# Moving the sliding-window attention out of the delta rule's recurrence and between the levels of its inverses, in a one-core Trainium2 transformer layer

## What is computed

```python
# attention: 8 heads of 64, 2 key/value heads, blocks of 128 queries over 256 keys
s = einsum('bnqhgd,bnkhd->bnhgqk', qb, kb) * HEAD_DIM ** -0.5        # masked to a window of 128
m = maximum(max(s, -1), sink);  p = exp(s - m)
o = einsum('bnhgqk,bnkhd->bnqhgd', p / (sum(p) + exp(sink - m)), vb) # then rms_norm * gain

# delta rule: 4 heads of 128, chunks of 64 tokens
a_mat = strict_lower((k*beta) @ k.T * decay) + I
u, w  = solve(a_mat, [v*beta, k*beta*exp(gc)])        # unit lower triangular, 64 x 64
for each chunk c:                                     # the recurrence, 8 chunks
    v_new = u[c] - w[c] @ state
    o[c]  = q_dec[c] @ state + qk[c] @ v_new
    state = state * decay[c] + k_dec[c].T @ v_new
```

## Time and profile before

| | |
|---|---|
| runs | 1737.12, 1762.24, 1736.94 us; median 1737.12 |
| the profiled execution | 1731.93 us; its span, first to last instruction, 1730.0 us |
| input projection, 0 to 163.0 | TensorE busy 144.1 us |
| `delta_prepare`, 163.0 to 264.2 (101.2 us) | busy: TensorE 77.0, VectorE 67.9, ScalarE 24.2, GpSimd 44.8; mean granted clock 0.85 |
| `mixers`, 264.2 to 373.8 (109.6 us) | busy: TensorE 91.1, VectorE 51.1, ScalarE 37.5, GpSimd 7.8; mean granted clock 0.74 |
| output projection, 373.8 to 495 | TensorE busy 111.8 us |
| routing 495 to 775, experts 775 to 1730 | TensorE busy 246.0 and 925.9 us |

### The profile page before, as it was taken

How to read it: one execution, slowest core, us unless ns; L and a number is a source line. 1 busy time by engine, 2 the same in 40 slices (tenths; PEclk the granted TensorE clock), 3 DMA queues, 4 the chain that set the end, 5 groups by cost and what they waited for, 6 DMA issues and landing times. The chain is left out here.

```text
span 1730.0 us, 23367 instructions
## 1 busy us (share of the span) xinstructions
PE 1595.9 (92%) x8745; PEld 1433.2 (83%) x8745; DVE 1310.7 (76%) x2258; ACT 715.5 (41%) x1388; POOL 342.0 (20%) x295
## 2 busy tenths in 40 slices
PE   6999498979988878999988899999999999999998
PEld 5899496758788878989988799999999988888886
DVE  4646944453269969899777788888888888999897
ACT  4544023352133356777756333333333333433332
POOL 4012720000036500020220221222122220110110
PEclk9999696879999999999999999999999999999999
DMA  4320002022125446768797997888888879999893
GB/s 160 98 75 2 1 1 105 1 97 86 61 88 151 145 121 181 215 200 301 220 331 253 403 377 291 349 311 304 328 331 339 332 257 412 342 360 367 333 364 111
DMA packets 147123, 380.82 MB, mean 220 GB/s; under 512 B 10449, under 2 KB 89425, under 8 KB 128337
## 3 DMA queue, kind: packets, MB, share of 16 engines
q1 hardware_dynamic: 118224, 231.17, 38.4%
q0 software_dynamic: 18432, 134.23, 19.9%
q10 hardware_dynamic: 10368, 14.16, 2.4%
HBM read 336.00 MB, written 43.52 MB: 219 GB/s over the span
## 5 line engine op out<-in xcount | busy, mean ns | idle before, releaser
L1342 POOL DMA_INDIRECT scores<-in_peer_uv,pair_index x86 | 125.7, 1462 | 631.6 <-DVE pair_sum L1366 467.4
L1926 PE MATMUL bank<-v_hi,act_hi 128*128 128x512 f32 x552 | 215.2, 390 | 5.0 <-DVE v_lo L1989 5.0
L1928 PE MATMUL bank<-v_hi,act_lo 128*128 128x512 f32 x552 | 215.8, 391 | 0.0
L1927 PE MATMUL bank<-v_lo,act_hi 128*128 128x512 f32 x552 | 215.7, 391 | 0.0
L1555 PE MATMUL bank<-x_hi,early_u_h 128*128 128x384 f32 x576 | 200.8, 349 | 16.0 <-POOL early_u_l L1486 15.8
L1556 PE MATMUL bank<-x_lo,early_u_h 128*128 128x384 f32 x576 | 195.6, 340 | 0.0
L1557 PE MATMUL bank<-x_hi,early_u_l 128*128 128x384 f32 x576 | 195.5, 339 | 0.0
L2002 DVE TENSOR_TENSOR act_tile<-gelu_tile,gate_tiles 128x384 f32<-128x384 f32 x128 | 117.5, 918 | 83.3 <-ACT gelu_tile L1974 70.8
L1914 PE MATMUL bank<-x_hi,u_split 128*128 128x384 f32 x448 | 151.3, 338 | 6.5 <-DVE u_split L1984 6.5
L1916 PE MATMUL bank<-x_hi,u_split 128*128 128x384 f32 x448 | 151.2, 338 | 0.0
L1915 PE MATMUL bank<-x_lo,u_split 128*128 128x384 f32 x448 | 151.0, 337 | 0.0
(11 more groups left out here) (315 smaller groups left out, 3744.4 us busy)
## 6 DMA issues: line engine op xcount, KB each, us to landing
v_raw<-in_peer_v SPq DMA_DIRECT2D x128, 512.0 KB
u_raw<-in_peer_u SPq DMA_DIRECT2D x64, 512.0 KB, 5.0
u_raw_more<-in_peer_u SPq DMA_DIRECT2D x64, 512.0 KB, 8.0
gates<-gate_stage SPq DMA_DIRECT2D x24, 1024.0 KB, 5.8
gate_tiles<-gates SPq DMA_DIRECT2D x16, 1536.0 KB, 15.2
early_gelus<-early_gelu ACTq DMA_DIRECT2D x72, 192.0 KB
gelu_tile<-early_gelus SPq DMA_DIRECT2D x72, 192.0 KB, 6.7
w_raw<-in_w_in SPq DMA_DIRECT2D x9, 1024.0 KB, 5.2
```

The lines of the kernel that those rows point to most:

```text
L1342: pool.indirect_dma_start(self.slot(k), None, self.table, bass.IndirectOffsetOnAxis(ap=self.sidx[:, k:k + 1], axis=0)).then_inc(self.lande ...
L1926: nc.tensor.matmul(bank[:], ah[:, s, w], v_hi[:, c], start=first, stop=False)
L1927: nc.tensor.matmul(bank[:], ah[:, s, w], v_lo[:, c], start=False, stop=False)
L1928: t = nc.tensor.matmul(bank[:], al[:, s, w], v_hi[:, c], start=False, stop=last)
```

## The change

The function `mixers` becomes `recurrence`, without the attention; `delta_prepare` becomes `prepare_mixers`, with it. The attention's arithmetic is the same. Its parts are put behind the parts of each level in every engine's list; its scores and transposes now share two PSUM banks and pass through them in turn, with one wait per pair of matmuls; its `pv` has one bank; the levels rotate over the remaining five. `v_beta` and `k_beta_decay` are written over `tok` in place. z's SiLU goes to the end of the preparation on ScalarE, its product with the gain into the even chunks. The recurrence's output gets two banks in turn. `mix` is allocated at the other end of SBUF.

```diff
-def delta_prepare(nc, m, ps, sem):
+def prepare_mixers(nc, m, ps, sem, sinks, att_out_g):
+    bA, bPV = ps[5:7], ps[7]
+    banks = Banks(ps[0:5], done, {"act": ..., "dve": ...})
...
-        vb = sb("v_beta", [P, DN, T])
-        kbe = sb("k_beta_decay", [P, DN, T])
+        vb, kbe = m.tok[:, 2 * DN:3 * DN, :], m.tok[:, DN:2 * DN, :]
...
+            @block.sync
+                sp.dma_start(snk[:], sinks...)
+                sp.dma_start(ag[:], att_out_g...)
...
             @block.tensor
+                def scores(b):
+                    lo = 0 if b else P
+                    for i in range(4):
+                        if i >= 2:
+                            pe.wait_ge(sc_out, 4 * b + i - 1)
+                        elif b:
+                            pe.wait_ge(p_out, 4 * b + i - 1)
...                         (two matmuls into bA[i % 2])
+                        t.then_inc(sc_done, 1)
+                def p_transposes(b):
+                    for i in range(4):
+                        pe.wait_ge(prob, NH * b + 2 * i + 2)
+                        if i < 2:
+                            pe.wait_ge(sc_out, 4 * b + i + 3)
+                        else:
+                            pe.wait_ge(p_out, 4 * b + i - 1)
...                         (four transposes, two for block 0, into bA[i % 2])
+                        t.then_inc(p_done, 1)
...             (behind kk and qkT, ahead of the level-0 transposes)
+                scores(0)
...             (in each level l, behind WT)
+                    if l >= 2:
+                        pv(l - 2)
...             (in each level l, behind Z and ZT)
+                    if l <= 4:
+                        p_transposes(l - 1)
+                    if l <= 3:
+                        scores(l)
...
             @block.scalar
...             (in each level l, behind the copies of WT)
+                    if l >= 3:
+                        att_square(l - 3)
+                    if l <= 4:
+                        probs(l - 1)
+                        pT_copies(l - 1)
...             (behind the copies of wT; att_square(TB - 1) behind the first)
+                nc.scalar.activation(m.z[:], m.z[:], ACT.Silu)
...
             @block.vector
...             (ahead of X and XT of level 0)
+                att_max(0)
...             (in each level l, behind X and XT)
+                    if l >= 3:
+                        att_norm(l - 3)
+                    if l >= 2:
+                        att_out(l - 2)
+                    if l <= 3:
+                        att_max(l)
...             (behind the copies of u)
+                att_norm(TB - 1)
...
-def mixers(nc, m, ps, sem, w_out_in, w_out, sinks, att_out_g, dn_out_g):
+def recurrence(nc, m, ps, sem, w_out_in, w_out, dn_out_g):
-    bV, bO, bS, bPV = ps[0], ps[1], ps[2], ps[3]
+    bV, bO, bS = ps[0], ps[1:3], ps[3]
...             (SyncE: the loads of sinks and att_gain go, that of dn_gain stays)
...             (TensorE)
-                scores(0)
...
-                    if q == 0:
-                        p_transposes(b)
-                    else:
-                        pv(b)
-                        if b + 1 < TB:
-                            scores(b + 1)
                     pe.wait_ge(v_new, c + 1)
...
-                    if c:
-                        pe.wait_ge(o_out, c)
+                    if c >= 2:
+                        pe.wait_ge(o_out, c - 1)
...             (VectorE)
                 nc.vector.memset(S[:, 0], 0.0).then_inc(zeroed, 1)
-                att_max(0)
-                dve.wait_ge(o_mix, 1)
-                dve.wait_ge(in_[2], 16)
...
+                dve.wait_ge(dg_in, 16)
                 for c in range(NC):
...                 (v_new)
-                    if q == 1:
-                        att_out(b)
-                        if b + 1 < TB:
-                            att_max(b + 1)
+                    if q == 0:
+                        z_gain(b)
```

## The result

| | before | after |
|---|---|---|
| median of the runs | 1735.08 us (1720.38 to 1762.24) | 1743.89 us (1738.02 to 1749.16) |
| ratio | | 1.0061, 95% interval 1.004 to 1.0082 |
| profiled execution | 1731.93 us, span 1730.0 | 1744.52 us, span 1742.8 |

The kernel became 0.6% slower. Ratios leave out executions over 1.5% above the quickest of their kernel, among them one of before of 2666.3 us beside the last four experiments.

What follows compares the result with a forecast made beforehand. TensorE was taken to set the pace in levels and mixers. Preparation +38.6 and recurrence stage -24.4 gave +14.2, added to a median of 1737.1: 1751.3 us, forecast 1751, 8-in-10 range 1735 to 1768.

Steps and rivals of the forecast that it cites:

- front: Start of the levels: X of level 0 begins later because scores(0) wait for VectorE's att_max(0); +4.5 us, bounds 3.5 and 7.
- `pv`: Levels 2 to 5: the attention's pv adds TensorE time, 1.9 for block 0 and 3.75 for each of three others; 13.2 us.
- transposes and scores: Levels 1 to 4: attention transposes and scores with handshakes add 4.8, 5.8, 5.8 and 2.3 on TensorE; 18.7 us together.
- end of the preparation: After the last level: ScalarE's SiLU with its table load runs past VectorE's end; +2.2 us.
- recurrence stage: Recurrence without attention: start 0.7, dn_gain wait 1.9, eight chunks 77.6, tail 5.0; 85.2 us against 109.6, so -24.4.
- clock: levels, recurrence: TensorE's granted clock: full (1.00) through the levels, 0.50 (1.2 GHz) through the recurrence until the output projection.
- at the output projection: Sum of the changes up to the output projection: preparation +38.6, recurrence stage -24.4, together +14.2 us.
- tail: From the recurrence's last output to the next block: 5.0 us, against 6.9 before.
- The prediction's frame: Whole kernel: nothing of the change reaches past the output projection, so a microsecond won or lost before 373.9 counts at the end.
- The fallen step: Recurrence: it starts at 1.2 GHz and stays there, since none of its matmuls has the 128*128 form that raised the clock.
- the rival: Recurrence at 2.4 GHz: chunks of 5.74 us, 31.7 us less, 1719.6 us, faster by 1.0%; chance 0.08.
- The rival by which the clock falls in the levels: Levels: handshakes, transposes or half-filled scores drop the clock to 1.2 GHz; 23 us more, 1774, slower by 2.1%; chance 0.06.

Runs made afterwards that it cites:

- e2_seam: After with z's SiLU moved into the last level and dn_gain loaded in the preparation; 1737.7 us, ratio 1.001 to before.
- e5_front: After with scores(0) put behind WT of level 1 and att_max(0) behind X and XT of level 0; 1739.7 us, ratio 1.005 to before.
- e6_all: After with the edits of e2_seam and e5_front, plus unread full matmuls: nine around the seam, three per chunk; 1705.4 us, ratio 0.9867 to before.
- e7_hoist: After with two heads' q·state products moved into TensorE's wait for v_new, no work added; 1707.6 us, ratio 0.9828 to before.
- e3_half: After with four unread half-filled matmuls (128*64) in each chunk's wait for v_new, from chunk 1 on; 1718.1 us, ratio 0.995 to before.
- e9_half_all: e6_all with every extra matmul half-filled, those in the chunks as in e3_half; 1707.5 us, ratio 0.985 to before.
- e1_chunk: After with three unread full matmuls per chunk from chunk 1 on, none at the seam; 1735.6 us, ratio 1.0004 to before.
- e4_before_fill: Before with unread full matmuls: 14 ahead of the first transposes, 10 ahead of w·state in chunks 2, 4 and 6; 1720.0 us, ratio 0.9945.
- e1_start: After with unread full matmuls at the seam and around the first w·state only, none in later chunks; 1724.0 us, ratio 0.9949 to before.
- e8_best: e6_all with e7_hoist's reordering in place of the three extra matmuls per chunk, the other nine staying; 1700.1 us, ratio 0.9781 to before.

## Why the prediction was right, step by step

| term | forecast | measured in after |
|---|---|---|
| front | +4.5 | +5.1 (Z of level 1 at 214.97, before at 209.51, less 0.35) |
| `pv` | 13.2 | 12.3 (1.73 + 3 x 3.52) |
| transposes and scores | 18.7 | 21.0 (5.66 + 6.52 + 6.52 + 2.33) |
| end of the preparation | +2.2 | +2.2 |
| recurrence stage | 85.2 | 84.5 |
| clock: levels, recurrence | 1.00, 0.50 | 1.00, 0.50 |
| at the output projection | +14.2 | +16.5, of which 0.35 was there ahead of the change |
| profiled execution | 1746.1 | 1744.5 |
| median of the runs | 1751.3 | 1743.9 |

The median was 7.4 us under its forecast. 1.6 of it is the profiled execution. The other 5.8 come of setting the change on the median of three runs, 5.2 above before's profiled execution; twenty runs put that median at 1735.1, and after's median lies 0.6 below its profiled execution. The mechanism has no part in this.

The mis-sized term is transposes and scores, 2.3 short. The time from the end of Z to the first scores is what was forecast (243.08 - 240.39 = 2.7 against 2.6). From there to the next WT it was 3.83 instead of 3.2: I let the fourth pair follow its bank at 5.0, and the sixteen records of the four pairs, 0.38 each as in before, were spread over 3.90, in pauses too short for the view to show as idle. That makes 0.7 in either of two levels, and 0.9 in level 1, whose handshake is 5.66 against 4.8. The measured terms of the preparation add up to 40.6 of the 41.2 us by which its end moved; the rest is WT behind scores, 3.68 instead of 3.57 in three levels, and the first Z behind `pv`. The recurrence came out nearly part for part: v_new of chunk 0 was 2.1 us late for `dn_gain` (1.9), chunks 9.68 (9.7), tail 5.1 (5.0); only the first w·state, forecast at 1.2 GHz, ran at 2.4 and gave 0.9 back. The 20.3 us that the prediction names for levels 2 and 3 does not fit its own terms for level 2, which has `pv` of block 0 alone: 10.72 + 1.9 + 5.8 = 18.4. Measured were 19.1 and 20.9.

Of the 16.5 us, 3.7 came back in stages whose code is unchanged, SyncE's timelines of before and of after:

```profile
435.76 0.43 SPq L1146 DMA_DIRECT2D h_spill<-acc  x1
...
625.19 6.96 SPq L1504 DMA_DIRECT2D u_raw<-in_peer_u  x2
```

```profile
451.31 0.43 SPq L1158 DMA_DIRECT2D h_spill<-acc  x1
...
638.03 6.96 SPq L1516 DMA_DIRECT2D u_raw<-in_peer_u  x2
```

That is +15.5 at the output projection's spill and +12.8 in the routing; from there the difference stays to the end. It is no gift of the change: from the start of the output projection to that issue in the routing took 251.4 us in before, 247.7 in after, 243.7 in e2_seam, 246.7 in e5_front, 244.7 in e6_all and 251.2 in e7_hoist, in no order that the edits explain. The prediction's frame, that a microsecond won ahead of 373.9 is one at the end, therefore holds only to within some 8 us in a single execution; that it offset the shortfall of the sum here, 12.6 against 14.2, is luck. What moves these stages I have not separated.

**The fallen step** is the reason for the slow recurrence. The prediction said that nothing in the block is "of the form that raised it", since all of it fills half the array or less. In e3_half and e7_hoist the clock rose with only such work in the block, and in e9_half_all it held. What these runs put in its place is the idle time in each chunk: with 0.78 us the clock stayed at 1.2 GHz for eight chunks; with the gap filled it came back in the second chunk (e3_half) or the third (e7_hoist, e1_chunk) of the profiled execution. The outcome was right, and so was the price of the alternative; the 0.08 for the rival was rightly low for this kernel as written, for the wrong reason. Beside it stands the Trainium skill, "TensorE: Matmul & The Clock Gate", section "Why this matters for your kernels", which wants TensorE busy continuously. I had said that the trace disagrees. For the recurrence it agrees: e7_hoist, whose TensorE has no break from 310.24 to 327.5, gets the clock back. For the stretch of before that follows it does not.

**What stays open.** Continuity is not all of it. In before TensorE had no gap at all from 274.77 to 301.4, 26.6 us, and stayed at 1.2 GHz; the last 19.6 us of it:

```profile
281.80:301.40 19.60, 19.60 (x72) 14.96 (x72) 8.06 (x16) 2.42 (x6) 0.35 (x2) 0.50 0.00 0
```

In that stretch ran `pv`, scores, kdec, outputs and w·state. Unbroken work of 8.9 us (e3_half), 17.2 (e7_hoist) and 21.3 (e1_chunk) stood ahead of a rise. Just ahead of the rises stood other work: transposes (4.07 us) in before, full fills in e4_before_fill, and w·state with fills or with q·state directly behind it in e3_half, e7_hoist and e1_chunk. But in e1_chunk the same unbroken w·state, fills and kdec did not raise the clock in the second chunk (from 317.20) and did in the third (from 327.62). Nor does the same code lose the clock at the same place: behind the same seam, 3.94 us idle, the first w·state took 1.09 us in after, 1.27 in e7_hoist and 1.97 in e1_chunk and e3_half. So what tells the unbroken stretch in before from the others, and one chunk from the next, is not settled by these runs; each was traced in one execution.

The rival by which the clock falls in the levels did not come about: 1.00 held from 212.4 to 305.7, through the transposes of four levels. The Trainium skill, "TensorE: Matmul & The Clock Gate", section "Part 4: PE-mode transpose", from which that rival had its support, says that they do not count as busy in the same way; here nothing came of it, with 1.3 to 2.2 us of transposes in a level, full matmuls ahead of them and scores (64\*128) or WT behind.

## What to carry over

When a slow clock prices a stage, look for the gap in its loop that TensorE spends waiting for another engine, and put into it work of the same iteration that is independent of the wait: here a reordering of two heads' products was worth some 36 us (1743.9 to 1707.6; by the stages of the profiled executions 84.5 to 54.8), about four times what moving the attention cost. A correlation between a rise of the clock and the form of one group of matmuls in one trace is a guess until a kernel with the form alone changed has run.

## What the runs showed of the hardware

- A loop of 5.84 us with one gap of 0.78 met the gap twice at 2.4 GHz and then lost the clock, at 324.6 (e1_start); with gaps of 0.35 in 4.98 it kept it for all eight chunks (e8_best).
- With the gaps filled, half-filled fills (128\*64) held the clock as full ones did: stages of 52.7 us (e9_half_all) and 52.8 (e6_all).
- 26.6 us of unbroken TensorE work can stay at 1.2 GHz (before, 274.8 to 301.4), and so did a stretch with 29.4 us busy of 30.6 (e4_before_fill).
- A VectorE operation on 128x8 elements took 0.17 us with GpSimd idle and 1.20 among GpSimd's level products (after, 206.32 and 250.78).
- The mean granted clock and the time of an execution of before go together: correlation -0.90 over 49 executions.
- `dn_gain` landed in 3.9 us (median, DMA issues of after) when it was first in the queue, 6.3 when it was third.
